# Packet size and cutting of the weight-sum transfers in the mixer half of a hybrid decoder layer

## What is computed

```
hn   = rmsnorm(x, norm1_g)
proj = hn @ w_in                                   # 1024 x 3608
q_a, k_a, v_a, gate_a, low_a, qkv_b, z_b, beta_b, dec_b = split(proj)
o_a, h_a = gla_chunked(q, k, v, log_a, state_gla)   # 4 heads, gated linear attention
qkv  = silu(causal_dwconv(qkv_b, state_conv, w4))
o_b, h_b = gdn_chunked(l2norm(q), l2norm(k), v, g, beta, state_gdn)   # 4 heads, gated delta rule
mix  = concat(rmsnorm(o_a) * silu(gate_a), rmsnorm(o_b) * silu(z_b))
x    = x + mix @ w_out                             # 1024 x 1024
hn2  = rmsnorm(x, norm2_g)
a, b = split(causal_dwconv(hn2 @ w_up, state_ffn, w3))   # w_up: 1024 x 5632
x    = x + (silu(a) * b) @ w_down                  # 2816 x 1024
y    = rmsnorm(x, norm_f_g)
```

## Time and profile before

| | us |
|---|---|
| median of 3 runs | 3193.25 (3193.14 to 3195.74) |
| profiled execution, its own time | 3197.49 |
| its span, first to last instruction | 3195.8 |
| PE busy in it | 3064.4 (96%) |
| DVE / ACT / POOL busy | 1832.6 / 926.4 / 328.1 |

### The profile page before, as it was taken

The page is one execution under the profiler, slowest core; times in us unless marked ns, Lnnn a source line. Parts: engine busy times, 40 slices in busy tenths (PEclk is TensorE's granted clock), DMA queues, the critical chain, the costliest instruction groups (busy, mean ns, idle before and its releaser), DMA issues. The chain is left out here.

```text
span 3195.8 us, 55638 instructions
## 1 busy us (share of the span) xinstructions
PE 3064.4 (96%) x21721; PEld 1983.5 (62%) x21721; DVE 1832.6 (57%) x4382; ACT 926.4 (29%) x2026; POOL 328.1 (10%) x609
## 2 busy tenths in 40 slices
PE   7999999999999999999679999989999999999998
PEld 3555655555655655555458888877888884444443
DVE  2566655556655556666576666677766674322223
ACT  2223332223322223322334434434444441000000
POOL 1111111111111111101110000000101010000000
PEclk9999999999999999999789999999999999999999
DMA  7276576676566654442567888774555567322211
GB/s 247 94 199 194 134 207 172 187 194 165 158 195 178 190 146 135 128 118 66 162 198 232 246 246 245 209 257 142 168 174 173 172 218 252 108 66 69 69 63 64
DMA packets 333763, 530.24 MB, mean 166 GB/s; under 512 B 23757, under 2 KB 252405, under 8 KB 319236
## 3 DMA queue, kind: packets, MB, share of 16 engines
q1 hardware_dynamic: 318531, 376.78, 36.7%
q0 software_dynamic: 11072, 86.51, 13.2%
q10 hardware_dynamic: 3904, 63.44, 5.4%
HBM read 473.57 MB, written 203.04 MB: 212 GB/s over the span
## 5 line engine op out<-in xcount | busy, mean ns | idle before, releaser
L758 PE MATMUL mixer_bank<-arena,hnt 128*128 128x451 f32 x2048 | 873.5, 558 | 15.2 <-DMA arena<-in_w_in_dram 8.2
L758 PEld LDWEIGHTS mixer_bank<-arena,hnt 128*128 128x128 f32 x2048 | 368.3, 192 | 304.9 <-issue 299.8
L2364 PE MATMUL mlp_psum<-mlp_room,arena 128*128 128x256 f32 (+1 forms) x1848 | 446.0, 386 | 17.4 <-DVE mlp_room L2761 5.8
L2364 PEld LDWEIGHTS mlp_psum<-mlp_room,arena 128*128 128x128 f32 x1848 | 353.5, 192 | 75.2 <-issue 6.6
L2364 PE MATMUL mlp_psum<-arena,mlp_room 128*128 128x256 f32 (+1 forms) x1320 | 328.2, 387 | 8.1 <-DVE arena L2766 8.1
L2364 PE MATMUL mlp_psum<-arena 128*128 128x256 f32 (+1 forms) x1144 | 284.2, 387 | 5.2 <-PEq L2997 4.8
L2364 PEld LDWEIGHTS mlp_psum<-arena,mlp_room 128*128 128x128 f32 x1320 | 253.6, 192 | 48.2 <-issue 8.5
L1218 ACT ACTIVATE proj<-mixer_bank,x_rs 128x451 f32<-128x451 f32 x128 | 81.3, 635 | 604.7 <-PE mixer_bank L758 572.7
L792 PE MATMUL mixer_bank<-wo,th 128*128 128x512 f32 x512 | 248.8, 609 | 2.5 <-DMA wo<-in_w_out_dram 1.8
L2364 PEld LDWEIGHTS mlp_psum<-arena 128*128 128x128 f32 x1144 | 219.4, 193 | 43.2 <-issue 7.3
L2453 PE MATMUL mlp_psum<-arena,mlp_room 128*128 128x512 f32 x560 | 242.9, 592 | 0.0
(11 more groups left out here) (405 smaller groups left out, 3913.6 us busy)
## 6 DMA issues: line engine op xcount, KB each, us to landing
wo<-in_w_out_dram SPq DMA_DIRECT2D x260, 256.0 KB, 2.9
arena<-q_blk SPq DMA_DIRECT2D x88, 512.0 KB, 4.5
mlp_room<-q_blk SPq DMA_DIRECT2D x66, 512.0 KB, 4.7
arena<-in_w_blk_dram SPq DMA_DIRECT2D x66, 384.0 KB, 3.5
arena<-s_blk SPq DMA_DIRECT2D x66, 384.0 KB, 3.4
q_blk<-s_blk POOLq DMA_DIRECT2D x8, 2816.0 KB, 20.1
t_blk<-in_d_blk_dram POOLq DMA_DIRECT2D x6, 2816.0 KB, 18.4
mlp_room<-act_t SPq DMA_DIRECT2D x28, 512.0 KB, 5.3
```

The source lines that it names most:

```text
L758: x = pe.matmul(bank[ring(g)][0:N, 0:GW], hnt[:, k, 0:N], w[:, k, g * GW:(g + 1) * GW], start=(k == 0), stop=(k == KT - 1))
L2364: x = pe.matmul(psum[:, bank, 0:N], weights[:, k * C:k * C + C], xb_of[block_of(n)][:, right, k, 0:N], start=(j in (1, 2, 5) and k == 0), ...
```

## The change

Views of the weight blocks are cut into rows of 512 elements (2 KB) instead of 2048, and the copies get the same limit. So every packet of the 12 copies and 12 accumulations is 2 KB; the bytes are the same. `pieces_of` cuts an accumulation into as many pieces as keep one at 30 rows for each DMA engine: 7 for an S sum, 5 for an R sum, 6 for a Q sum (72 in all, 24 before; 768 to 960 KB each). Pieces 0 and 1 are issued where the first half was, piece 2 behind level 0, 3 behind level 2, 4 behind level 4, 5 and 6 behind level 6. Each piece now waits until the one before it has landed.

```diff
-STASHED = 32 * 12
+PIECE_ROWS = 30
+STASHED = 16 * 72
...
-            return v.rearrange("s i p c -> s (i p c)").rearrange("s (a b) -> a s b", b=2048)
+            return v.rearrange("s i p c -> s (i p c)").rearrange("s (a b) -> a s b", b=512)
...
+        def pieces_of(n):
+
+            shape = STASH_SUMS[n][1].shape
+            return -(-(shape[0] // 16) // (PIECE_ROWS // math.prod(shape[1:-1])))
+
+        def pieces_before(n):
+            return sum(pieces_of(i) for i in range(n))
...
             def stash_sum(t, part):
 
                 for n, (at_, dst, src) in enumerate(STASH_SUMS):
-                    if at_ == t:
-                        half = dst.shape[0] // 32 * 16
-                        r = slice(half, dst.shape[0]) if part else slice(0, half)
+                    if at_ == t and part < pieces_of(n):
+                        r0, r1 = (dst.shape[0] // 16 * k // pieces_of(n) * 16 for k in (part, part + 1))
+                        before = pieces_before(n) + part
                         if part == 0:
                             gp.wait_ge(s_wo_used, 16 * t)
                             gp.wait_ge(s_stash_copied, 16 * (n + 1))
-                            if n:
-                                gp.wait_ge(s_stash_added, 32 * n)
-                        gp.dma_start(dst[r], src[r], accum_op=ALU.add, max_dma_last_dim=8192)\
+                        if before:
+                            gp.wait_ge(s_stash_added, 16 * before)
+                        gp.dma_start(dst[r0:r1], src[r0:r1], accum_op=ALU.add, max_dma_last_dim=2048)\
                             .then_inc(s_stash_added, 16)
...
                 stash_sum(t, 0)
+                stash_sum(t, 1)
...
-                    if a == 2:
-                        stash_sum(t, 1)
+                    for part, level_at in enumerate((0, 2, 4, 6, 6)):
+                        if a == level_at:
+                            stash_sum(t, 2 + part)
...
                         if sums:
-                            act.wait_ge(s_stash_added, 32 * sums)
-                        act.dma_start(dst, src).then_inc(s_stash_copied, 16)
+                            act.wait_ge(s_stash_added, 16 * pieces_before(sums))
+                        act.dma_start(dst, src, max_dma_last_dim=2048).then_inc(s_stash_copied, 16)
```

More of the change, by code:

```diff
@@ L382, in inner @@
         def inner(blk, n):
-            v = [blk[j, 0:n].rearrange("o i p c -> (o i p c)").rearrange("(a b) -> a b", b=2048) for j in range(4)]
+            v = [blk[j, 0:n].rearrange("o i p c -> (o i p c)").rearrange("(a b) -> a b", b=512) for j in range(4)]
             return v
@@ L388, in mixers @@
         R1, R2, R3, R4 = inner(q_blk, 3)
-        Q1, Q2, Q3, Q4 = (q_blk[j, 3:7].rearrange("o i p c -> (o i p c)").rearrange("(a b) -> a b", b=2048)
+        Q1, Q2, Q3, Q4 = (q_blk[j, 3:7].rearrange("o i p c -> (o i p c)").rearrange("(a b) -> a b", b=512)
                           for j in range(4))
@@ L570, in _ @@
             sp.wait_ge(s_stash_copied, 16 * len(STASH_COPIES))
-            sp.wait_ge(s_stash_added, 32 * len(STASH_SUMS))
+            sp.wait_ge(s_stash_added, STASHED)
             sp.dma_start(sum_w[0], q_blk[:, WEIGHT_OF[0], 0].rearrange("s p c -> p s c")).then_inc(s_sum[0], 16)
```

## The result

The changed kernel takes **3199.89 us** (median; 3194.94 to 3207.57) against 3188.41 us for the kernel before in the same runs (3181.38 to 3195.74; the three runs shown first are among them). The ratio is 1.0036, 95% interval 1.0024 to 1.0047: slower by a little, where 3153 and faster were forecast. One caution for the traces: the profiled execution of after is its fastest (3194.94, span 3192.9), and that of before is one of its slowest (3197.49), so what is read from the two traces alone is 14 us too kind to the change.

What follows compares the result with a forecast made beforehand. PE was taken to bound the kernel, stopped by late instruction packets. Gain 42.2 less 2 us for lateness makes 40 us off the 3193.25 median: 3153 us, range 3142 to 3176.

Steps and rivals of the forecast that it cites:

- What bounds the kernel, and what was lost there: PE sets the time; late instruction packets behind large DMA packets cost 51.3 us in 13 mixer tiles.
- the quiet tile: The tile without copy or accumulation, 91.62 us at full clock, from which the other 13 tiles' excess was counted.
- Packets of 2 KB: On the DMA engines, a copy packet should take about 0.105 us, an accumulation packet 0.17, with 0.34 as far end.
- Another factor 4 in size should bring it to some 0.7: Excess per mixer tile falls from 1.8 us at 8 KB to 0.7 at 2 KB; 42.2 us gained, between 27.9 and 51.3.
- The price of 1.8 times a wait's length: Each PE issue wait costs about 1.8 times its length, since PE runs at a lower clock behind the stop.
- The pieces on POOL: Waits for 5 to 7 accumulation pieces fit POOL's idle stretches at cost 0; 2 us in all allowed for lateness.
- POOL comes too late: Rival: accumulation packets at twice the proportion or more make piece waits outlast POOL's idle stretches; 60 us slower, 3213; chance 0.04.
- ACT: The copy's single issue on ACT, 176 rows an engine, stays at about 0.5 us; extra cost taken at 0.
- The rival that had ACT stand: Rival: ACT blocks issuing the 176-row copy, as SP did for 24.30 us; PE loses 154 us, 3307; chance 0.06.
- Size only to 8 KB: Rival: packets below 8 KB gain nothing more, all 13 tiles keep 1.8 us excess; 3168; chance 0.17.
- It does nothing: Rival: bytes in flight, which stay the same, hold up the instruction queue; time within 6 of 3193; chance 0.07.
- The signs named: Profile signs: right, issue waits under 6 us; wrong, 2 to 3 us at L993, ACT issue over 10, PE waiting for POOL.

Runs made afterwards that it cites:

- the shifted kernel: Kernel before with copies in 2 KB packets, plus 21 more transposes in the prologue, which moves all later PE instructions by 42 places; 3174.69 us (0.9949).

## Why the prediction was wrong, point by point

*What bounds the kernel, and what was lost there.* Right in the main. PE bounds, and the stops come with background work: the run without copy and accumulation beside the dense part has no issue wait at all. But the quiet tile is not the same work (1062 matmuls, 88.77 us of PE, against 994). In the run with 2 KB copies and no accumulations the eleventh tile, which then has neither, takes 92.02 us and the thirteenth 91.87. So some 5 of the 51.3 us were never there to be gained. The cause, late instruction packets, was an inference; the shifted kernel bears it out, since nothing but the instructions' places was changed, and two stops moved by exactly the 21 matmuls.

*Packets of 2 KB.* Right in kind, and the durations come near. DMA view (packets, MB, share of 16 engines) of the kernel with 2 KB copies and no accumulations, 592 to 602 us:

```profile
q10 hardware_dynamic: 1502, 3.07, 87.8%
```

A packet takes 0.878 x 10 x 16 / 1502 = 0.094 us (0.105 forecast). An accumulation's takes 0.725 x 8.1 x 16 / 464 = 0.20 us, the 16 semaphore writes left out (0.17 forecast, 0.34 the far end), in the changed kernel from 1370.3 to 1378.4 us:

```profile
q0 software_dynamic: 480, 0.95, 72.5%
```

*"Another factor 4 in size should bring it to some 0.7", 42.2 us.* **Too large.** With 2 KB copies the 13 tiles are 748.09 + 464.09 - 13 x 91.62 = 21.1 us over the quiet tile instead of 9.1, and the medians moved by 28.6 and 22.7 us. The rate was taken from 8 KB tiles and continued to nothing, as if all of it were size. Of the 12 us between, some 5 are the quiet tile's lighter work, which no packet size gives back. 11.3 of the 21.1 us are the second, fifth and eighth tile (96.45, 94.32 and 95.34 us), whose stops stay with packets of any size tried. The price of 1.8 times a wait's length was somewhat high too: less the 5 us that were never lost, it is 46 / 29.0 = 1.6 in the kernel before and 16 / 11.8 = 1.4 with 2 KB copies.

*The pieces on POOL, "cost 0 ... 2 us in all".* **This is the step that failed.** The change lies 31 us above the same pieces with twice the room and no waits between them (3199.9 to 3168.4) and 27 above the same pieces elsewhere (3172.5). In its trace PE is 24.7 us late behind POOL: the 15.8 us at the second level and the 8.9 on the masked matrix. Two things went wrong in it. A landing was put at "some 7 us" and beside the copy at 10.3; the five pieces of the seventh tile land 10.8, 7.3, 8.0, 14.0 and 12.8 us after their issue, the first beside a `resid` store, the last two beside the copy. And each piece was held against the idle stretch in front of its own place only. But they are a chain: "piece 1 waits for piece 0 in an idle stretch of 13.66 us: hidden" is true, yet it goes out at 766.55, lands at 774, and piece 2, put at 771, can go out only then, at 774.26. The masked matrix of the second level stands behind it. The condition of the rival "POOL comes too late" (an accumulation packet at twice the proportion) was not met, and POOL was late all the same. Its price, 60 us, was too high, its chance of 0.04 far too low.

*The two together.* The forecast is a ratio of 0.987, measured is 1.0036: 52 us apart. Of these, 14 to 20 are the gain that was put too high (42.2 against the 28.6 and 22.7 measured), and the other 32 to 38 are the pieces, put at 2.

The Trainium skill, "DMA: Bandwidth & Descriptors", "Anatomy of one DMA", puts 2.0 us on each software transfer. By an estimate from that figure 48 more cost 96 us. Measured, they cost some 34 us with the change's places (3199.9 against 3166), 6 with the others (3172.5) and 2 with room for two (3168.4), the smaller packets of the accumulations included. What was paid was not a price for each but the wait at particular places.

*ACT.* Right: 0.49 us. The rival that had ACT stand read the 24.30 us of SP as a queue that couldn't take more rows. No run shows that for SP's queue: with the same 44 KB copy and no accumulations the seventh tile's `xt` load issues in 0.35 us, and with 2 KB copies and 8 KB accumulations in 7.45. What held it stays open. *Size only to 8 KB:* wrong, 9 us lie below 8 KB. *It does nothing:* wrong in its reason, though the measured time lies 7 us from its 3193: a gain and a larger loss came out near nothing, which is luck.

*The signs named.* Two of what would show it wrong came: POOL released by DMA with PE waiting for POOL (though with accumulation packets at 0.20 us, not over 0.3), and issue waits of over 2 us in the same places (2.21 and 2.25 us in the second and fifth tile).

**The best version** is the one with 2 KB copies and untouched accumulations: 0.9909 and 0.9934 in two sets of runs, better than both kernels. The kernels with pieces and room for two, or with 4 KB halves, are level with it and more complicated.

## What to carry to other kernels

A chain of transfers on an engine that also computes has to be followed as a chain: add up landing after landing, at the durations of a busy stretch, and compare each issue with the work behind it. Free all locks together before calling a wait harmless (here the semaphore and the queue's room were two), and when a loss is extrapolated to zero along one cause, first look for a tile where it stays for another.

## What the runs showed that was not expected

- With the room of 1024 bytes a piece of 26 rows an engine holds POOL at the next issue until it has landed, without any wait in the program that isn't met: 11.3 us between two issues, 0.3 us behind the landing. With twice the room two issues take 2.05 us together in the seventh tile; in the fourth, with an S sum, the second still goes out 10.1 us behind the first.
- Copies in 2 KB packets are no gentle neighbours of `wo`'s loads (larger packets were not tried at that place). `wo` chunks landed in 2.9 us; with the copy ahead of them (the run with both copies and accumulations, the six chunks issued from 774 to 795 us) the view of the tile `wo` has

```profile
DMA to landing us min/median/max: 2.4/13.1/15.5
```

  and PE lost up to 8.8 us in a tile to them.

- A stop of PE at fixed places of the instruction stream (the last 6, 10 and 13 matmuls of a block, every third tile) moved with 21 more transposes in the prologue, where it could be followed by 21 matmuls. The place of an instruction in the program is part of its cost where the stream is dense and the DMA engines are busy. Whether copies throttled to a part of the engines' time would end these stops was not tried.
